# A cache stage whose keys are turned by VectorE and whose pages all come through SyncE's queue

## The reference

```python
past_k = cache_k[l][page_table].reshape(nb_s, n_pages * PAGE_SIZE, MOBA_HEADS, MOBA_HD)
past_v = cache_v[l][page_table].reshape(nb_s, n_pages * PAGE_SIZE, MOBA_HEADS, MOBA_HD)
...
gate = jnp.einsum('bqhd,bjhd->bhqj', qq.astype(jnp.float32), k_mean)
gate = jnp.where(blk_ids[None, None, None, :] < own[None, None, :, None], gate, -jnp.inf)
_, top = lax.top_k(gate, n_sel)
...
logits = jnp.einsum('bqhd,bhqsnd->bqhsn', qq, kg).astype(jnp.float32) * scale
logits = jnp.where(mask, logits, -jnp.inf).reshape(B, H, qc, -1)
p = jax.nn.softmax(logits, axis=-1).reshape(mask.shape).astype(v.dtype)
return jnp.einsum('bhqsn,bhqsnd->bqhd', p, vg)
```

## Time and profile before

| | before |
| --- | --- |
| median of 3 runs | 1468.2 us (1467.29 to 1468.88) |
| the profiled execution | 1469.78 us, span of the profile 1468.1 us |
| TensorE busy | 1434.4 us, 98% of the span |
| VectorE busy | 571.9 us, 39% |
| ScalarE busy | 259.0 us, 18% |
| GpSimd busy | 43.4 us, 3% |
| moved by DMA | 515.28 MB, 351 GB/s over the span |
| cache stage on TensorE, first scores to last output | 336.4 to 445.1 us |
| expert loop | from about 519 us to the end |

### The profile page before, as it was taken

The page is one execution under the profiler, slowest core; times in us unless marked ns, Lnnn a source line. Parts: engine busy times, 40 slices in busy tenths (PEclk is TensorE's granted clock), DMA queues, the critical chain, the costliest instruction groups (busy, mean ns, idle before and its releaser), DMA issues.

```text
span 1468.1 us, 20188 instructions
## 1 busy us (share of the span) xinstructions
PE 1434.4 (98%) x7694; PEld 637.7 (43%) x7694; DVE 571.9 (39%) x1220; ACT 259.0 (18%) x541; POOL 43.4 (3%) x85
## 2 busy tenths in 40 slices
PE   7999999999999999999999999999999999999996
PEld 3644575677777733333333333333333333333332
DVE  4016625424543563334324433432343233323334
ACT  2103034546530231000001000100000010001001
POOL 1100000012320000000000000000000000000000
PEclk9999999999999999999999999999999999999998
DMA  9646447667967498999999999999999999999994
GB/s 363 226 168 229 173 155 252 224 235 247 336 227 282 162 379 333 421 429 428 429 428 429 429 429 429 428 429 429 429 429 429 429 429 428 429 429 429 429 429 201
DMA packets 75283, 515.28 MB, mean 351 GB/s; under 512 B 6259, under 2 KB 15401, under 8 KB 47586
## 3 DMA queue, kind: packets, MB, share of 16 engines
q1 hardware_dynamic: 69682, 497.44, 83.1%
q0 software_dynamic: 5552, 17.16, 3.3%
HBM read 507.24 MB, written 7.34 MB: 351 GB/s over the span
## 4 chain that ended last, share of the span: by engine, by line
PE 41%; DMA 21%; DVE 1%; issue 0%; SPq 0%; DVEq 0%
PE ps L1155 21%; DMA ring<-in_w_gate_up 21%; PE ps L1174 10%; PE ps L1121 3%; PE ps L1185 3%; PE ps L584 2%; PE ps L1137 1%; PE ps L1188 1%; DVE mem L2209 0%; DVE mem L2197 0%; SPq L511 0%; DVE mem L2102 0%; DVE mem L2174 0%; DVE mem L2105 0%; DVE mem L2117 0%
## 5 line engine op out<-in xcount | busy, mean ns | idle before, releaser
L1155 PE MATMUL ps<-ring,mem 128*64 128x512 f32 x2032 | 445.7, 594 | 5.0 <-DMA ring<-in_w_gate_up 4.9
L1155 PEld LDWEIGHTS ps<-ring,mem 128*64 128x64 f32 x2032 | 142.1, 137 | 306.3 <-issue 289.5
L1174 PE MATMUL ps<-ring,mem 128*64 128x512 f32 x1024 | 227.4, 597 | 0.0
L2098 DVE TENSOR_SCALAR mem<-ps 128x512 f32<-128x512 f32 x32 | 22.1, 692 | 413.2 <-PE ps L1155 413.2
L1174 PEld LDWEIGHTS ps<-ring,mem 128*64 128x64 f32 x1024 | 70.8, 137 | 152.6 <-issue 152.6
L2116 DVE TENSOR_TENSOR mem<-ps,mem 128x1024 f32<-128x1024 f32 (+1 forms) x97 | 101.2, 1043 | 40.7 <-PE ps L1185 28.7
L1506 ACT ACTIVATE mem<-mem 128x512 f32<-128x512 f32 x32 | 20.2, 630 | 490.2 <-DVE mem L2098 490.2
L2117 DVE TENSOR_TENSOR mem<-mem 128x1024 f32<-128x1024 f32 (+1 forms) x97 | 101.2, 1043 | 3.3
L1121 PE MATMUL ps<-mem 128*64 128x512 f32 (+1 forms) x384 | 92.7, 600 | 1.3 <-issue 1.3
L584 PEld LDWEIGHTS ps<-mem 128*128 128x128 f32 (+2 forms) x487 | 63.6, 179 | 69.4 <-issue 54.5
L584 PE MATMUL ps<-mem 128*128 128x128 f32 (+2 forms) x487 | 85.7, 303 | 6.0 <-DMA mem<-in_x_sample 2.3
(11 more groups left out here) (352 smaller groups left out, 1140.5 us busy)
## 6 DMA issues: line engine op xcount, KB each, us to landing
ring<-in_w_gate_up SPq DMA_DIRECT2D x127, 2048.0 KB, 20.2
ring<-in_w_down SPq DMA_DIRECT2D x64, 2048.0 KB, 18.8
ring<-in_w_ada SPq DMA_DIRECT2D x12, 2048.0 KB, 11.1
ring<-in_w_in SPq DMA_DIRECT2D x12, 2048.0 KB, 11.4
ring<-in_cache_k SPq DMA_DIRECT2D x64, 256.0 KB, 4.7
ring<-in_cache_v POOLq DMA_DIRECT2D x64, 256.0 KB, 5.4
ring<-in_state_gla SPq DMA_DIRECT2D x2, 2048.0 KB, 9.2
out<-ring SPq DMA_DIRECT2D x2, 2048.0 KB, 10.9
```

The source lines that it names most:

```text
L1155: last = mm(out, xeT[:, 2 * (s % 2) + k, s // 2, :], w[:, k, 512 * q:512 * q + 512], start=False, stop=s == 3 and k == 1)
L1174: last = mm(ps[64 * f:64 * f + 64, 0, :], actT[:, k, s, :], w[:, k, 512 * f:512 * f + 512], start=s == 0 and k == 0, stop=s == 1 and k == 3)
L2098: v.tensor_scalar(glu, ps[:, 2, :], LIMIT, None, ALU.min).then_inc(glu_sb, 1)
```

## The change

**SyncE and GpSimd.** All pages are issued by SyncE, and GpSimd's part is gone. The loops are written out. The order is keys 0, values 0, keys 1, values 1, the second half of w_proj_gla (which now goes to a place `aux2`, free once the prompt's attention is over), then keys 2, keys 3, values 2, keys 4, values 3, and so on to keys 7, values 6, values 7, and then w_proj_moba and w_out. Keys of b wait for the scores of b - 2, values of b for the values of b - 2.

**Keys.** TensorE no longer turns keys, and ScalarE no longer copies them. VectorE turns them where they lie, in pieces of 32x32 (`keys_turned`): four instructions a sequence, each for 32 of the 128 dimensions of every head pair. After it, a group of 32 partitions holds 32 tokens' keys with the dimension along the partitions. The scores become products with 32 rows and 32 columns: for each of four dimension groups g, four head pairs p and four token groups i one product of 256 columns, added up over g. The queries must stand in all four groups of partitions for that; `queries_spread` does it once by TensorE for all sequences, and ScalarE fills in those of a sequence (`cache_queries`).

**Order of a turn.** TensorE's turn b is one whole projection by w_proj_gla (all eight are in the turns now, `turn_project`), values of b - 1, scores of b + 1 (which wait until the exponentials of b have been read from the same banks), the output of b - 1, and the probabilities of b. ScalarE takes over the copies of the probabilities, the scaling and the copying of the output from VectorE.

```diff
         for b in range(NB):
-            used[N_CACHE + 2 * b], used[N_CACHE + 2 * b + 1] = (kt2_ps, 8 * b + 8), (co_ps, b + 1)
-        for j, jobs in enumerate((8, 16, 20, 24)):
+            used[N_CACHE + 2 * b], used[N_CACHE + 2 * b + 1] = (cs_ps, b + 1), (co_ps, b + 1)
+        for j, jobs in enumerate((16, 20, 24)):
             used[N_PROJ + j] = (pj_ps, jobs)
...
+            def value_pages(b):
+
+                n = N_CACHE + 2 * (b % 2) + 1
+                for j in range(NPAGES):
+                    page = sp.value_load(ptab[0:1, bass.ds(b * NPAGES + j, 1)], min_val=0, max_val=cache_k.shape[1] - 1)
+                    sp.dma_start(item(n)[:, j, :], v_pages[bass.ds(page, 1)].rearrange("o s n -> s (o n)")).then_inc(v_land[b % 2], 16)
+
             for b in range(2):
                 sp.wait_ge(*used[N_CACHE + 2 * b - PRE])
                 key_pages(b, b)
-            with sp.Fori(1, NB // 2) as i:
-                for par in range(2):
-                    b = i * 2 + par
-                    sp.wait_ge(kt2_ps, b * 8 - 8)
-                    sp.sem_inc(turns, 1)
-                    key_pages(b, par)
+                sp.wait_ge(*used[N_CACHE + 2 * b + 1 - PRE])
+                value_pages(b)
+            sp.wait_ge(mot_ps, 1)
+            sp.dma_start(aux2, w_proj_gla[0][:, 512:1024].rearrange("(k p) n -> p k n", p=P)).then_inc(side_in, 16)
+            for b in range(2, NB + 1):
+                if b < NB:
+                    sp.wait_ge(cs_ps, b - 1)
+                    key_pages(b, b % 2)
+                if b > 2:
+                    sp.wait_ge(co_ps, b - 2)
+                    value_pages(b - 1)
             for n in range(N_PROJ, N_PRE):
                 load(n)
...
             def cache_scores(b):
 
-                pe.wait_ge(kt2_sb, b * 8 + 8)
-                pe.wait_ge(q_sb, b + 1)
-                for f in range(2):
+                keys = item(N_CACHE + 2 * (b % 2))
+                pe.wait_ge(qz_sb, b + 1)
+                for g in range(4):
+                    pe.wait_ge(kb_sb, 4 * b + g + 1)
                     for p in range(PAIRS):
-                        mm(ps[32 * p:32 * p + 32, 4 + f, :], qs[:, p, :], kTs[:, p, 512 * f:512 * f + 512], start=True, stop=True)
+                        c0 = p * P + 32 * g
+                        for i in range(4):
+                            rows = slice(32 * i, 32 * i + 32)
+                            mm(ps[32 * p:32 * p + 32, 4 + i, 0:BLOCK], qz[rows, g, p, :], keys[rows, :, c0:c0 + 32],
+                               start=g == 0, stop=g == 3)
...
-            for b in range(1, NB - 1):
-                cache_turn(b, b // 2, b % 2)
...
+            for b in range(NB):
+                turn_project(b)
+                if b:
+                    pe.wait_ge(cp_sb, b)
+                    pe.wait_ge(cot_sb, b)
+                    cache_values(b - 1)
+                pe.wait_ge(cs_exp, b + 1)
+                if b + 1 < NB:
+                    cache_scores(b + 1)
+                if b:
+                    cache_out(b - 1)
+                cache_probs(b)
...
+            def keys_turned(b, pieces):
+
+                nk = N_CACHE + 2 * (b % 2)
+                dve.wait_ge(land[nk % PRE], b // 2 * (16 * NPAGES) + landed[nk])
+                for j in pieces:
+                    x = ring[:, nk % PRE, :].rearrange("p (a g d) -> p a g d", g=4, d=32)[:, :, j, :]
+                    v.transpose(x, x).then_inc(kb_sb, 1)
...
+            for b in range(NB):
                 cache_max(b)
+                if b + 1 < NB:
+                    keys_turned(b + 1, range(4))
+                else:
+                    dve.wait_ge(qz_sb, NB)
+                    shifts()
+                projected(b)
+                cache_den(b)
...
-            pool.wait_ge(pt_in, 16)
-            def value_pages(b, par):
-                n = N_CACHE + 2 * par + 1
-                for j in range(NPAGES):
-                    page = pool.value_load(ptab[0:1, bass.ds(b * NPAGES + j, 1)], min_val=0, max_val=cache_k.shape[1] - 1)
-                    pool.dma_start(item(n)[:, j, :], v_pages[bass.ds(page, 1)].rearrange("o s n -> s (o n)")).then_inc(v_land[par], 16)
```

More of the change, by code:

```diff
@@ L212, in decoder_layer @@
         om_tok = part(mem, g0 + 2304, 2, MH * HD)
-        kTs = part(mem, g0, PAIRS, PAGE * NPAGES)
+        aux2 = part(mem, g0, KD, 512)
         pex = part(mem, g0 + 4096, PAGE * NPAGES + NS_TOK)
         pts = part(mem, g0 + 5184, NPAGES, P)
+        q_rep = part(late, 5120, 4, PAIRS, NS_TOK)
         pto = part(mem, g0 + 6208, P)
@@ L218, in decoder_layer @@
         osm = part(mem, g0 + 6464, P)
+        qz = part(mem, g0 + 6592, 4, PAIRS, 32)
         e0 = g0 + 7168
@@ L380, in decoder_layer @@
             w2d[N_GR[c]], w2d[N_BA + c], w2d[N_BA + 2 + c] = (w_in2, C_GR + 512 * c), (w_in2, C_BA + 512 * c), (w_in2, C_BB + 512 * c)
-        for n, w, c0 in ((N_PROJ, w_proj_gla, 512), (N_PROJ + 2, w_out, 0), (N_PROJ + 3, w_out, 512)):
+        for n, w, c0 in ((N_PROJ + 1, w_out, 0), (N_PROJ + 2, w_out, 512)):
             w2d[n] = (w[0], c0)
@@ L843, in gate_bank @@
             def gate_bank(n):
-                return n % 2 if n < 42 else 3
+                return n % 2
             def prompt_scores(p):
@@ L904, in _, with queries_spread @@
             gate_steps(42, gate_bank(42), 4, KD)
[L907 to L924, removed]
+            def queries_spread():
+                pe.wait_ge(mo_sb, MH)
+                for g in range(4):
+                    for i in range(4):
+                        last = mm(ps[32 * i:32 * i + 32, 6 + g // 2, BLOCK * (g % 2):BLOCK * (g % 2 + 1)], ident[:, 32 * g:32 * g + 32],
+                                  mqT[:, :, NP_TOK:T], start=True, stop=True)
+                last.then_inc(qr_ps, 1)
@@ new lines, in cache_out @@
+            def cache_out(b):
+                act.wait_ge(cot_ps, b + 1)
+                for hh in range(2):
+                    rows = slice(64 * hh, 64 * hh + 64)
+                    src = ps[rows, 2, 0:P].rearrange("p (a r) -> p a r", r=32)[:, :, 8 * hh:8 * hh + 8]
+                    last = a.copy(oTm[rows, :, NP_TOK + LS * b:NP_TOK + LS * b + LS], src)
+                last.then_inc(cot_sb, 1)
+            gate(42)
+            act.wait_ge(qr_ps, 1)
+            for f in range(2):
+                a.copy(q_rep[:, 2 * f:2 * f + 2], ps[:, 6 + f, :].rearrange("p (g a b) -> p g a b", g=2, b=NS_TOK)).then_inc(act_step, 1)
@@ L1449, in _ @@
+            act.wait_ge(act_step, 17)
+            cache_queries(0)
             gate(43)
-            cache_keys(1)
+            cache_queries(1)
+            gate(44)
             cache_exp(0)
-            cache_keys(2)
-            gate(44)
-            cache_exp(1)
-            with act.Fori(2, NB - 1) as b:
-                cache_keys(b + 1)
-                cache_exp(b)
-            cache_exp(NB - 1)
+            probs_copied(0)
+            for b in range(1, NB):
+                if b + 1 < NB:
+                    cache_queries(b + 1)
+                cache_exp(b)
+                cache_scale(b - 1)
+                cache_out(b - 1)
+                probs_copied(b)
@@ L1930, in projected @@
                 dve.wait_ge(pj_ps, n + 1)
-                bank = ps[:, 3, 0:T] if n < 4 else ps[:, n % 4, 0:T]
+                bank = ps[:, 3 if n < 8 else n % 4, 0:T]
                 if which == 0:
@@ L1983, in _ @@
             link(v.memset(lg, 0.0))
-            for n in range(7, 24):
+            for n in range(8, 24):
                 projected(n)
@@ L2201, in _ @@
             dve.wait_ge(last_sb, 1)
-            second().then_inc(x3_sb[2], 1)
+            second().then_inc(x3_sb, 1)
             for t in range(3):
```

225 lines of the change are left out of this document (89 added, 136 removed).

## The result

| | before | after |
| --- | --- | --- |
| median of the runs | 1468.2 us (1467.29 to 1468.88, 4 runs) | 1492.8 us (1488.93 to 1497.43, 4 runs) |
| ratio, 95% interval | | 1.0169 [1.014, 1.0199] |
| the profiled execution | 1469.78 us, span 1468.1 | 1492.58 us, span 1490.8 |
| projection 8 starts | 449.4 us | 471.9 us |
| projections end | 501.3 us | 526.8 us |

The change costs 24.6 us. The forecast was 17.6 us more, 1486 in a range of 1477 to 1500. The two profiled spans lie only 22.7 us apart: the profiled execution of the kernel before ran 1.6 us over its median, that of the kernel after 0.2 us under its own.

A forecast was written before the change was run, and what follows sets the result against it. TensorE bounded the kernel before; SyncE's page queue would bound the cache stage after. 340.1 + 8.9 + 0.4 + 106.6 + 9.3 + 1.7 puts projection 8 at 467.0 against 449.4, +17.6 us: 1486, range 1477 to 1500.

The forecast's parts named there:

- The deciding term: Cache stage, SyncE's queue: sixteen page issues of 1.11 us, 17.8 us a turn against TensorE's 9.7 and VectorE's 10.3.
- first page of values 1 issued: SyncE's queue: values 1 wait for gate 44, which was to end at 340.1 us.
- twelve items: SyncE's queue behind w_proj_gla's second half: 96 pages at 1.11 us, 106.6 us, ending at 456.0.
- w_proj_moba, issue to use: Weight load queued behind the last value page: 9.3 us from issue to landing, to 465.3.
- clock at the restart: TensorE at projection 8: one half-clock stretch after the thin stage adds 1.7 us, to 467.0.
- Transposes: VectorE in the cache stage: four key transposes of 1024 columns at 1.2 us each, 4.8 us a turn.
- Scores: TensorE in the cache stage: 64 products on 32x32 pieces, sixteen side by side, 2.0 us; 7.8 if four.
- The other arm: Stage end: last values land 4.7 us after 456.0, then 2.1 of values and 1.6 of output, to 464.4.
- The queue keeps up: Rival, cache stage: pages under 0.6 us on SyncE leave TensorE setting the turn, 1439 us; chance 0.09.
- Half clock through the stage: Rival, cache stage: TensorE at 1.2 GHz throughout, turns of 19.4 us, about 1504 us; chance 0.04.
- Transposes are dear: Rival, VectorE: transposes decide from 3.1 us each; at 6.9 the loss is over 100 us; chance 0.02.
- It cancels: Rival, SyncE: overlapping page instructions, 0.85 us a page gives 9 us faster, 0.95 no change; in between 0.03.

The follow-up runs named there:

- e3: Kernel after with page numbers as program constants instead of read from the table, so other pages are attended to: 1457.45 us, 0.9923 of before.
- e7: Kernel after with the number of each value page read twice from the table on SyncE: 1520.84 us, 1.0357 of before.
- e1: Kernel after with value pages back on GpSimd's queue, all else the same: 1455.75 us, 0.9911 of before.
- e4: Kernel after with w_proj_moba loaded ahead of the value pages of sequence 7 instead of behind them: 1493.71 us, 1.0162 of before.
- e5: Kernel after with TensorE's idle time in turns 1 to 6 and before projection 8 filled with unread products: 1490.63 us, 1.016 of before.
- e8: Kernel after with w_proj_moba loaded ahead of values 6, two items earlier: 1485.25 us, 1.0118 of before.
- e9: Version with value pages on GpSimd, with neighbouring score products on different 32x32 pieces of TensorE: 1456.37 us, 0.9926 of before.

## Why the prediction was right, and where its sizes were off

*The deciding term.* "The cover is gone; the queue becomes the bound" holds. 1.10 us a page stands in the trace after; e3 takes more than half of it away and gets nearly the gain of the moved keys, e7 raises it and the time follows, e1 moves half of it and the loss becomes a gain.

*The sum, link by link.* All five of its links came out somewhat longer:

| link | forecast | measured | more |
| --- | --- | --- | --- |
| first page of values 1 issued | 340.1 | 342.44 | 2.3 |
| values 1 and half of w_proj_gla | 9.3 us | 9.7 us, to 352.12 | 0.4 |
| twelve items | 106.6 us | 109.3 us, to 461.4 | 2.7 |
| w_proj_moba, issue to use | 9.3 us | 10.5 us, to 471.9 | 1.2 |
| clock at the restart | 1.7 us | 54.89 - 51.84 = 3.05 us | 1.35 |

Together 7.9: 17.6 became 25.5 at the end of the projections, of which some 3 came back in routing and tail. The first link is long by scores 0 (2.7 for 2.0, and 0.25 for the new keys), by 0.75 us between gate 44's end and the first issue, which I had left out, and by some 0.6 in the gates. The third is an item's distance, 352.12 to 461.38 in twelve: 9.1 us where I took 8.88, since eight pages sometimes take 8.4 to 9.8 us. The last two I took from a landing and from a low stretch seen once each; both were lower bounds here. What came back later was no term of the sum, and the half of it in the tail is luck of the two executions. The turns were forecast at 17 to 18 us; in the trace they are 12.5 to 20.5, because keys 2 come late on the queue and keys 3 right behind them. That changes nothing in the sum, which follows the queue.

*The operations that no row showed.* Transposes: 1.2 us forecast, 1.212 measured, so the product of equal size was the right neighbour and the reciprocal the wrong one. Scores: 2.0 forecast, 2.7 at full clock, between the bounds of 2.0 and 7.8 and near the lower; it matters little while the queue is the path, and 0.7 us a turn once it isn't.

*The other arm.* I had the last output ready at 464.4, 0.9 before w_proj_moba. It was ready near 469, 3 us before it; its values ran at the lower clock, 3.57 instead of 1.95 us. The arms are that close, so moving the weight can win 2 to 3 us of start at most, and e4 lost them again on values 7.

*Rivals.* "The queue keeps up" was priced at 1439, for a page under 0.6 us. e3 meets that condition at first with 0.47 us and took 1457.45; e1, where two queues keep up, took 1455.75. In e1 projection 8 starts 13.0 us later than I had it: 9.0 of them in six turns of 11.2 us and not 9.7 (scores 0.7 more, the rest in small pieces and short waits), 3.2 behind the last scores and 0.8 ahead of them. "Half clock through the stage" fell: four of the seven groups of scores from 346 us on run at the lower clock, three don't, and the queue hides it (e5). But the row that I held against it was misread: busy stretches do not hold 1.00 in every row, the second window of the earlier trace rows is busy for all of its 3.40 us at 0.50. GpSimd's queue is also hardly the dearer one: the 1.23 us were a page of its loop, and written out, in e1, its pages stand 1.13 to 1.14 us apart. "Transposes are dear" fell by 1.212 us. "It cancels" needed 0.95 us a page.

What stays open: what holds some pages on the queue for longer than 1.10 us, why e8's other three executions are some 4 us under its profiled one, and the kernel after's spread by 8.5 us. In the kernel after, spans and clocks go together (1487.1 at 0.986, 1490.8 and 1491.1 at 0.984, 1495.6 at 0.979), which is no proof of cause.

## What to carry to other kernels

A queue's work is instructions, not bytes: count what each transfer needs on the issuing engine, register reads included, and set it against the turn that it must hide in, before moving transfers from one engine to another. When a stage gets shorter on its bounding engine, the next bound can be such a queue, as here, and it must shrink in step. A large transfer behind a string of small ones waits for all of them, and put ahead, it delays those right behind it: here the 2 MB of w_proj_moba gained nothing eight pages ahead of the end of the string, and 7.5 us sixteen pages ahead.

## What was new in the runs

- A transfer whose page number comes from a table costs 1.10 us on SyncE's queue, one with a constant number 0.47 while the queue has no other wait, and a second read of the number 0.50.
- VectorE turns 128x1024 fp32 numbers in 32x32 pieces, in place, in 1.212 us.
- 64 score products of 256 columns on 32x32 pieces (128 records) take 2.7 us at full clock, in either order of the pieces (e1, e9), about 1.4 times the 1.92 us of the 8 products of 512 columns that they replace.
